# Expert layers of a diffusion trunk: the down weights issued from GpSimd instead of SyncE

## What is computed

```python
def moe_ffn(h, router, w_gu, w_down):
    logits = (h @ router).astype(jnp.float32)
    top_v, top_i = lax.top_k(logits, TOP_K)
    w = jax.nn.softmax(top_v, axis=-1)
    combine = jnp.sum(jax.nn.one_hot(top_i, N_EXPERTS, dtype=jnp.float32) * w[..., None], axis=-2)
    gu = jnp.einsum('btd,edf->btef', h, w_gu)
    g, u = jnp.split(gu, 2, axis=-1)
    act = jax.nn.silu(g) * u * combine[..., None].astype(h.dtype)
    return jnp.einsum('btef,efd->btd', act, w_down)
```

## Time and profile before

| | us |
|---|---|
| median of three executions | 2205.32 |
| the profiled execution | 2205.23 |
| its span | 2203.4 |
| PE busy | 2112.8 (96%) |
| mean rate of all transfers | 250 GB/s |
| bytes moved | 550.91 MB |
| queue q1 (SP), share of the 16 DMA engines | 60.6% |
| queue q0 (POOL), share of the 16 DMA engines | 10.6% |
| queue q10 (ACT), share of the 16 DMA engines | 0.6% |

### The profile page before, as it was taken

One profiled execution on the slowest core, in us unless ns is written; L12 is line 12 of the kernel. 1 busy time (PEld: TensorE's weight loads), 2 busy tenths in 40 slices (PEclk: granted clock), 3 DMA queues, 4 the chain that ended last, 5 costly groups with the idle time before them and its releaser, 6 DMA issues.

```text
span 2203.4 us, 44096 instructions
## 1 busy us (share of the span) xinstructions
PE 2112.8 (96%) x19281; PEld 1541.4 (70%) x19281; DVE 776.9 (35%) x1728; ACT 387.1 (18%) x812; POOL 127.1 (6%) x221
## 2 busy tenths in 40 slices
PE   6998989999999999989999999999998999999898
PEld 4776878888888544535687788888887875455355
DVE  2235745777422301000312355572337633010003
ACT  1124441000101110000222210002144431100000
POOL 3100011111000000000100011110000000000000
PEclk8999999999999999999999999999999999999999
DMA  8964049987456699999485799753441058999992
GB/s 331 283 241 134 13 125 343 342 295 248 153 178 214 250 372 395 394 396 394 156 257 187 247 341 296 239 177 103 138 134 34 13 208 301 369 396 397 396 397 113
DMA packets 377288, 550.91 MB, mean 250 GB/s; under 512 B 13201, under 2 KB 329489, under 8 KB 371777
## 3 DMA queue, kind: packets, MB, share of 16 engines
q1 hardware_dynamic: 349600, 466.59, 60.6%
q0 software_dynamic: 21968, 76.84, 10.6%
q10 hardware_dynamic: 5536, 4.73, 0.6%
HBM read 537.64 MB, written 14.93 MB: 251 GB/s over the span
## 4 chain that ended last, share of the span: by engine, by line
PE 73%; SPq 15%; DVE 6%; issue 2%; DMA 2%; ACT 2%; ACTq 0%; DVEq 0%
PE ps L684 71%; SPq L502 10%; SPq L506 3%; SPq L526 2%; DMA ring<-in_moe_w_gu 1%; DVE ring L2129 1%; DVE ring L2123 1%; ACT ring L1555 1%; DVE ring L2104 1%; DVE ring L2148 1%; DVE work L1962 0%; ACT work L1555 0%; PE ps L870 0%; DMA ring<-in_ada_w 0%; PE ps L1128 0%
## 5 line engine op out<-in xcount | busy, mean ns | idle before, releaser
L684 PE MATMUL ps<-hT,ring 128*128 128x256 f32 x3200 | 716.2, 382 | 2.9 <-DVE hT L1972 2.5
L684 PE MATMUL ps<-ring,work 128*32 128x352 f32 (+5 forms) x7864 | 666.5, 443 | 28.4 <-DMA ring<-in_moe_w_gu 16.2
L684 PEld LDWEIGHTS ps<-hT,ring 128*128 128x128 f32 x3200 | 609.4, 191 | 115.4 <-issue 21.4
L684 PEld LDWEIGHTS ps<-ring,work 128*32 128x32 f32 (+2 forms) x7864 | 324.9, 115 | 340.4 <-issue 235.3
L1555 ACT ACTIVATE work<-ps 128x256 f32<-128x256 f32 (+10 forms) x238 | 107.5, 454 | 1290.3 <-PE ps L684 1021.3
L684 PE MATMUL ps<-work,ring 128*128 128x256 f32 (+1 forms) x1344 | 283.5, 369 | 0.2 <-DVE work L2196 0.2
L684 PEld LDWEIGHTS ps<-work,ring 128*128 128x128 f32 (+1 forms) x1344 | 238.0, 185 | 33.6 <-issue 1.1
L2551 DVE SCALAR_TENSOR_TENSOR work<-work,csil 128x1024 f32<-128x1024 f32 x196 | 239.7, 1279 | 42.4 <-DMA work<-in_ada_w 41.8
L2445 DVE TENSOR_TENSOR work<-work,ps 96x352 f32<-96x352 f32 (+2 forms) x80 | 41.6, 520 | 374.6 <-PE ps L684 374.1
L684 PE MATMUL ps<-ring 64*64 64x64 f32 (+1 forms) x4192 | 153.5, 236 | 17.6 <-DVE ring L2148 8.5
L684 PEld LDWEIGHTS ps<-ring 64*64 64x64 f32 x4192 | 130.4, 139 | 32.7 <-DVE ring L2148 13.4
(11 more groups left out here) (264 smaller groups left out, 1061.5 us busy)
## 6 DMA issues: line engine op xcount, KB each, us to landing
ring<-in_moe_w_gu SPq DMA_DIRECT2D x128, 1408.0 KB, 13.8
work<-in_ada_w POOLq DMA_DIRECT2D x112, 512.0 KB, 6.4
ring<-in_moe_w_down SPq DMA_DIRECT2D x48, 1024.0 KB, 12.9
ring<-in_ff_w_gu SPq DMA_DIRECT2D x88, 512.0 KB, 7.6
ring<-in_ada_w SPq DMA_DIRECT2D x40, 1024.0 KB, 8.6
ring<-in_dn_w_in SPq DMA_DIRECT2D x32, 1024.0 KB, 5.5
ring<-in_moe_w_down SPq DMA_DIRECT2D x64, 512.0 KB, 11.6
ring<-in_ff_w_down SPq DMA_DIRECT2D x44, 512.0 KB, 9.4
```

Source lines behind the costliest of these rows:

```text
L684: return pe.matmul(out, lhsT, rhs, start=start, stop=stop, **kw)
```

## The change

A helper `expert_down(eng, l, e, j)` issues the DMAs of one down piece from the engine given. SP no longer issues pieces 8, 9, 10 and `SPARES`, neither for expert 0 nor in the loop, and no longer waits for `p_dn` in the loop. POOL issues them: those of expert 0 after one wait for the latest freed slot (and in layer 3 for the scratch area), then a loop for the loads of rounds 1 to 6, each piece after its own wait for `p_dn`. After that come the wait for `y_out`, the gathers, and a second loop for the loads of round 7 and any further wide round. The bytes, the slots and all other engines' programs stay.

```diff
--- before.py
+++ after.py
@@ -345,6 +345,30 @@
         GATE_COL = [0, HALF, PW, HALF + PW]
         ROWS = [64, 64, 64, 64, 73, 24, 2, 73]
 
+        def expert_down(eng, l, e, j):
+            dn, at = a["moe_w_down"][l // 2], PLAN.moe_slot[l]
+
+            def down(c, n, x):
+                eng.dma_start(ring[:, at[j], x * DM:(x + n) * DM].rearrange("p (c n) -> p c n", c=n),
+                              dn[e, c * P:(c + n) * P, :].rearrange("e (c p) n -> p (e c) n", p=P)) \
+                    .then_inc(moe_in[j], 16)
+
+            if j == 8:
+                down(0, 2, 0)
+                down(6, 1, 2)
+            elif j == 9:
+                down(7, 1, 0)
+                down(2, 2, 1)
+            elif j == 10:
+                down(4, 2, 0)
+                down(8, 1, 2)
+            else:
+                for c, g, n in ((0, 0, 3), (0, 3, 1), (1, 0, 4)):
+                    row, s = (9 + c) * P, at[4 * c + g]
+                    eng.dma_start(ring[:, s:s + n, SPARE:SLOT],
+                                  dn[e, row:row + P, QUARTER * g:QUARTER * (g + n)]
+                                  .rearrange("e p (g n) -> p (e g) n", n=QUARTER)).then_inc(moe_in[j], 16)
+
         def last_in(j):
 
             return 3 if j >= 3 else {0: 2, 1: 2, 2: 5}[j]
@@ -495,38 +519,17 @@
                              dn[bass.ds(c, P), :])
 
                 def expert(e, j):
-                    gu, dn = a["moe_w_gu"][l // 2], a["moe_w_down"][l // 2]
+                    gu = a["moe_w_gu"][l // 2]
                     e, at = bass.ds(e, 1), PLAN.moe_slot[l]
 
                     def columns(c):
                         sp.dma_start(ring[:, at[j], 0:SPARE].rearrange("p (k n) -> p k n", k=KC),
                                      gu[e, :, c:c + PW].rearrange("e (k p) n -> p (e k) n", p=P)).then_inc(moe_in[j], 16)
-
-                    def down(c, n, x):
-                        sp.dma_start(ring[:, at[j], x * DM:(x + n) * DM].rearrange("p (c n) -> p c n", c=n),
-                                     dn[e, c * P:(c + n) * P, :].rearrange("e (c p) n -> p (e c) n", p=P)) \
-                            .then_inc(moe_in[j], 16)
 
                     if j in GATE:
                         columns(GATE_COL[j])
                     elif j in UP:
                         columns(DFE + GATE_COL[j - 4])
-                    elif j == 8:
-                        down(0, 2, 0)
-                        down(6, 1, 2)
-                    elif j == 9:
-                        down(7, 1, 0)
-                        down(2, 2, 1)
-                    elif j == 10:
-                        down(4, 2, 0)
-                        down(8, 1, 2)
-                    else:
-                        for c, g, n in ((0, 0, 3), (0, 3, 1), (1, 0, 4)):
-                            row, s = (9 + c) * P, at[4 * c + g]
-                            sp.dma_start(ring[:, s:s + n, SPARE:SLOT],
-                                         dn[e, row:row + P, QUARTER * g:QUARTER * (g + n)]
-                                         .rearrange("e p (g n) -> p (e g) n", n=QUARTER)).then_inc(moe_in[j], 16)
-
                 if l % 2 == 0:
                     for j in range(SLOTS):
                         slot_free(n0 + j)
@@ -539,18 +542,15 @@
                     for j in range(SLOTS):
                         if PLAN.moe_before[l][j]:
                             free(*PLAN.moe_before[l][j])
-                        expert(0, j)
-                    expert(0, SPARES)
+                        if j not in DOWN:
+                            expert(0, j)
                     sp.wait_ge(moe["d_np"], l // 2 + 1)
                     n_last = sp.value_load(rounds[0:1, 0:1], min_val=1, max_val=1 + EXTRA)
                     n_more = sp.snap(n_last + (NARROW - 1))
                     with sp.Fori(0, n_more) as r:
                         e = sp.value_load(order_e[0:1, bass.ds(r + 1, 1)], min_val=0, max_val=NE - 1)
-                        for j in (0, 1, 3, 2, 4, 5, 7, 6, 8, 9, 10, SPARES):
-                            if j in DOWN + [SPARES]:
-                                sp.wait_ge(moe["p_dn"], (done[0] + r) * 4 + (j - 7))
-                            else:
-                                sp.wait_ge(moe["p_gu"], (done[0] + r) * 8 + (j + 1))
+                        for j in (0, 1, 3, 2, 4, 5, 7, 6):
+                            sp.wait_ge(moe["p_gu"], (done[0] + r) * 8 + (j + 1))
                             expert(e, j)
                     done[0] = sp.snap(done[0] + n_more + 1)
             sp.wait_ge(d_fin, 2)
@@ -625,6 +625,24 @@
                                               bass.IndirectOffsetOnAxis(ap=rows_at[:, g, x:x + 1], axis=0)) \
                             .then_inc(landed[g], 16)
 
+                po.wait_ge(unit_done, max(m for kind, m in PLAN.moe_before[l] if kind == "unit") + 1)
+                if l == 3:
+                    po.wait_ge(d_mix, 12)
+                    for out in state_out:
+                        po.wait_ge(out, 128)
+                for j in DOWN + [SPARES]:
+                    expert_down(po, l, slice(0, 1), j)
+                po.wait_ge(moe["d_np"], i + 1)
+                n_last = po.value_load(rounds[0:1, 0:1], min_val=1, max_val=1 + EXTRA)
+
+                def next_down(r):
+                    e = po.value_load(order_e[0:1, bass.ds(r + 1, 1)], min_val=0, max_val=NE - 1)
+                    for j in DOWN + [SPARES]:
+                        po.wait_ge(moe["p_dn"], (done[0] + r) * 4 + (j - 7))
+                        expert_down(po, l, bass.ds(e, 1), j)
+
+                with po.Fori(0, NARROW - 1) as r:
+                    next_down(r)
                 po.wait_ge(moe["y_out"], (i + 1) * NARROW * 64 + 64)
                 po.tensor_tensor(tick[0:1, :], iota[0:1, 0:1], iota[0:1, 0:1], ALU.mult).then_inc(moe["o_but"], 1)
                 po.wait_ge(moe["d_idx"], i + 1)
@@ -632,6 +650,9 @@
                 po.wait_ge(filled, 16 * RND)
                 fetch(y_lo, 1, [moe["lo_in"]] * 2)
                 fetch(y_hi, 0, [moe["hi_in0"], moe["hi_in1"]])
+                with po.Fori(NARROW - 1, n_last + (NARROW - 1)) as r:
+                    next_down(r)
+                done[0] = po.snap(done[0] + n_last + NARROW)
 
             po.wait_ge(unit_done, PLAN.first[0]["in"][0] + 1)
             po.memset(rpb_sb[0:48, :], 0.0).then_inc(o_z, 1)
```

## The result

| | before | after |
|---|---|---|
| median, us | 2205.99 (2202.1 to 2207.14, 4 executions) | 2238.71 (2231.79 to 2241.49, 4 executions) |
| ratio to before | | 1.0142, 95% interval 1.0121 to 1.0164 |
| profiled execution, us | 2205.23 | 2231.79 |
| its span, us | 2203.4 | 2230.1 |

The kernel is slower by 32.7 us (1.4%); 2237.6 was forecast.

What follows compares the result with a forecast made beforehand. The prediction took full DMA engines, not SP's issue, as the bound in the expert rounds. Per layer 14.5 us for order plus 1.7 us of clock, two layers 32.4 us, on 2205.2 gave 2237.6 us, range 2214 to 2251.

Steps and rivals of the forecast that it cites:

- The bound: Expert rounds: DMA engines full at 398 GB/s, 43.5 us per expert against PE's 40; SP's issue is no limit.
- Parts costed at nothing: SP's removed DMAs, POOL's nine issues per round, expert 0's down pieces and round 7's down loads: no cost.
- The turns by packet: DMA engines serve both queues one packet for one packet, so waiting down pieces take 74% of the rate.
- 14.5 us for the order: Round 6's first up step: its seventh gate/up piece comes 14.5 us later, behind 5.77 MB of down.
- 1.7 us of clock per layer: Waits at rounds 4 and 6 instead of one: one more clock dip of 1.7 us, bounds 0 and 3.4.
- The sum: Two expert layers: 16.2 us each, 32.4 us together, giving 2237.6 us.
- Where the waits would be: PE's gate/up waits grow from 8 to about 22 us per layer, over rounds 4 and 6, few at 2.
- When the down pieces are asked for: Round 6: POOL asks for all down pieces by 971 us; all down bytes are through by about 993 us.
- The sign "before 975 us": Sign that the forecast is right: POOL's down issues of round 6 stand before 975 us.
- The rivals: Whole kernel: faster, 2186 us, chance 0.06; no change, 2205 us, 0.10; much slower, 2261 us, 0.06.
- two queues keep the engines fuller: Faster rival: round 6's wait goes away, 19 us saved, needing 440 GB/s with the order lost; chance 0.06.

Runs made afterwards that it cites:

- one-loop run: Changed kernel with round 7's down loads moved into POOL's first loop, ahead of the tick and the gathers: 2234.51 us, ratio 1.0138 to the kernel before.
- the repeat: The changed kernel measured once more, nothing altered: 2236.66 us, ratio 1.0136 to the kernel before.
- the version with half the bytes: Changed kernel, but POOL issues only pieces 8 and 9, SP again 10 and SPARES behind its gate/up pieces: 2218.49 us, ratio 1.0060 to before.

## Why the prediction was right, point by point

- **The bound.** Right. From 788 to 1000 us the eight traces move 392 to 398 GB/s on the mean, and SP's share of the chain was the pace of the data. Taking 12 points of SP from the chain made the kernel slower. The stream wasn't full "all the way", though: from 745 to 788 us it is 361 GB/s before and 362 after.
- **Parts costed at nothing.** Right. POOL's nine issues take about 6 us of a round. Expert 0, round 7 and GpSimd's path cost nothing that can be told from zero (holding the pieces back gave 1.0012, at most 1.0025; one loop changed nothing).
- **The turns by packet.** Right, 1138 against 1139.
- **14.5 us for the order.** Right in kind, and somewhat too large. Round 6's first up step starts at 1005.93 us; before it started at 977.97 + 25.60 - 9.67 = 993.9 us. That is 12.0 us of the 14.5 forecast, and 13.0 us in layer 3, counted from the start of that layer's experts. Two things make up the difference in layer 1. PE wasn't ready for the seventh piece at 992.4 us, as forecast, but at 993.9: the forecast took three gate steps at the full clock. The piece landed at 978.3 + 14.7 = 993.0 us (rows below, the later of the two), so the first 0.9 us of its lateness cost nothing. And it came 12.9 us later with the change, not 14.5. From 734 us to its landing 105.62 MB had moved after and 100.14 before, so 5.48 MB more and not 5.77, at a mean rate of 388 instead of 387 GB/s. In the two other traces with all down pieces unheld (the one-loop run and the repeat) PE's first up step of round 6 comes 12.8 to 14.0 us later (from the start of each layer's experts), so the 12.0 is itself at the low end. The sixth and seventh gate/up piece of round 6 on SP before, issue and landing:

```profile
L502 SPq DMA_DIRECT2D ring<-in_moe_w_gu x2: 3317/3320/3322, 974.7 to 978.3; - x2
...
DMA to landing us min/median/max: 13.9/14.3/14.7
```

- **1.7 us of clock per layer.** Right in size, for another reason than the one given. The prediction counted a dip at round 4 beside that at round 6. The run that held back round 6 alone shows that what PE loses at rounds 2 and 4 isn't added, be it a wait or a slow step. What adds is where round 6's slow step lies. Before, it was in the gate steps, and half of its 1.7 us PE would have stood waiting for the seventh piece anyway. Now it is in the up steps themselves, which take 11.01 us in layer 1 and 12.40 in layer 3 instead of 9.67. That is 1.3 and 2.7 us.
- **The sum.** PE enters the wide round 13.7 us later in layer 1 and 16.5 in layer 3 (from the start of that layer's experts; 16.2 each was forecast): 12.0 + 1.3 + 0.3 and 13.0 + 2.7 + 0.7, where the last term is a longer gap before the wide round. The span grew by 26.7, less than the 30.2 of the two layers, since the stretch from layer 1's wide round to layer 3's first expert took 797.6 us instead of 801.5, at a mean granted clock of 0.99 instead of 0.98. The executions of one kernel differ by 5 to 10 us, so it is luck that the median, 32.7 us, lies so near to the forecast of 32.4.
- **Where the waits would be.** 22 us per layer were forecast, at rounds 4 and 6 and a few at 2. They are 18.5 and 19.0 us, and round 2 has a full share, 5.2 us.
- **When the down pieces are asked for.** The sign "before 975 us" failed: it was 976.91 to 987.8 us, and q0 had moved them by about 1002 us, not 993. The prediction took PE's down steps of round 5 from the trace of before, where they start at 958.58 us. Rounds 2 and 4 had by then held PE up, and they start at 973.45 us. It changed nothing in the sum: the seventh gate/up piece was issued at 976.7 us and the down bytes still got ahead of it.
- **The rivals.** None of the three came true. That two queues keep the engines fuller isn't borne out. The 405 GB/s of the mixed stretch are far from the 440 needed, and one queue alone reached more before the change, where down pieces were moving:

```profile
764.00:770.00 6.00, 6.00 (x102) 3.53 (x101) 0.00 (x0) 0.57 (x1) 0.00 (x0) 1.00 1.05 411
```

## What to carry to other kernels

When the DMA engines are full, ask in which order the bytes are needed before asking who issues them. Here one queue whose order was the order of use was worth 1.4% more than two of which one ran ahead. The turns by packet gave 73% of the bytes to the stream that was needed later, because its packets were the larger ones; how much smaller packets would have saved wasn't tried. If a second queue is wanted for other reasons, hold its requests back until the urgent stream is through; and look at the single queue's own order at the place of the wait, here worth 0.4% for two pairs of pieces swapped in one round.

## What was not expected

Holding the down pieces back spread PE's one long wait over five short ones of 0.6 to 2.8 us with nearly the same sum, and the time stayed at 1.0012. And in the version with half the bytes the long waits went back to the first gate step, though the total grew; why wasn't tried.
